# In each attention step of the first block, VectorE reads out the finished head and copies the turned probabilities ahead of the row maximum of the step's scores

## The reference

```
h = rms_norm(x); proj = h @ w_in
6 heads:  softmax(q k^T / 8 + c[t] - c[s]) v          (forget gates, causal)
4 heads:  (softmax(q1 k1^T) - lam softmax(q2 k2^T)) v (causal)
6 heads:  softmax over the 128 keys with the largest index score, times a shared v
x = x + concat(heads) @ w_out
x = x + (silu(h' @ w_gate) * (h' @ w_up)) @ w_down,   h' = rms_norm(x)
```

## Time and profile before

| | |
|---|---|
| median of 3 runs | 2273.99 us (2273.98 to 11201.12) |
| profiled execution | 2271.32 us, its span 2269.5 us |
| PE busy | 2063.1 us, 91% of the span |
| DVE / ACT / POOL busy | 1230.1 / 854.6 / 518.6 us |
| mean granted PE clock | 0.952 of full speed |
| attention steps, first layer | about 102 to 391 us |
| attention steps, second layer | about 862 to 1152 us |

### The profile page before, as it was taken

One profiled execution on the slowest core, in us unless ns is written; L12 is line 12 of the kernel. 1 busy time (PEld: TensorE's weight loads), 2 busy tenths in 40 slices (PEclk: granted clock), 3 DMA queues, 4 the chain that ended last, 5 costly groups with the idle time before them and its releaser, 6 DMA issues. The chain is left out here.

```text
span 2269.5 us, 30334 instructions
## 1 busy us (share of the span) xinstructions
PE 2063.1 (91%) x11592; PEld 1760.0 (78%) x11592; DVE 1230.1 (54%) x2338; ACT 854.6 (38%) x1402; POOL 518.6 (23%) x355
## 2 busy tenths in 40 slices
PE   6988898899999999798989999999799989789994
PEld 6887777788888788786768888888788878777773
DVE  3676453544454447745554444538962233479885
ACT  4444433421222344343442212214224552267762
POOL 2654321000000136532110000004365535200001
PEclk9999988999999999898989999999999999799997
DMA  4111100412221111110123122205346543489995
GB/s 154 57 57 38 42 25 19 176 59 108 111 103 64 38 61 57 38 38 28 38 99 133 63 104 111 100 11 160 72 124 190 153 139 112 166 326 404 402 380 214
DMA packets 61627, 270.95 MB, mean 119 GB/s; under 512 B 15040, under 2 KB 19904, under 8 KB 37056
## 3 DMA queue, kind: packets, MB, share of 16 engines
q1 hardware_dynamic: 52864, 237.84, 30.1%
q10 hardware_dynamic: 6048, 22.02, 2.5%
q0 software_dynamic: 2592, 9.44, 1.1%
HBM read 244.14 MB, written 37.19 MB: 124 GB/s over the span
## 5 line engine op out<-in xcount | busy, mean ns | idle before, releaser
L1241 PE MATMUL fill_ps<-w_hi,h_hi 128*128 128x256 f32 (+1 forms) x704 | 213.1, 303 | 13.9 <-ACT values L866 5.2
L1241 PE MATMUL fill_ps<-w_hi,h_lo 128*128 128x256 f32 (+1 forms) x704 | 203.7, 289 | 0.0
L1241 PE MATMUL fill_ps<-w_lo,h_hi 128*128 128x256 f32 (+1 forms) x704 | 203.2, 289 | 0.0
L795 POOL TENSOR_TENSOR w_lo<-w_raw,w_hi 128x1024 fp32r<-128x1024 f32 x60 | 151.7, 2539 | 193.5 <-ACT w_hi L858 192.7
L322 POOL TENSOR_SCALAR norm_ss<-norm_ss 128x1 f32<-128x1 f32 x24 | 4.9, 202 | 798.6 <-ACT ffn_raw_d L316 738.2
L516 DVE TENSOR_TENSOR ffn_silu<-ffn_silu,ffn_up 128x512 f32<-128x512 f32 x44 | 30.2, 687 | 285.9 <-ACT ffn_silu L474 285.9
L1241 PEld LDWEIGHTS fill_ps<-w_hi,h_hi 128*128 128x128 f32 x704 | 140.6, 200 | 27.1 <-issue 16.1
L528 DVE TENSOR_TENSOR x<-ffn_down,x 128x512 f32<-128x512 f32 x176 | 119.1, 689 | 71.2 <-PE ffn_down L590 70.4
L1321 PEld LDWEIGHTS o_ps<-values,prob_t 128*128 128x128 f32 x800 | 111.7, 201 | 57.4 <-DVE prob_t L1100 46.9
L1707 POOL TENSOR_TENSOR w_lo<-w_raw,w_hi 128x1024 fp32r<-128x1024 f32 x48 | 126.0, 2642 | 131.3 <-ACT w_hi L1814 131.3
L575 PE MATMUL ffn_up<-h_hi,w_hi 128*128 128x512 f32 x384 | 152.1, 396 | 3.7 <-PEq L772 3.7
(11 more groups left out here) (456 smaller groups left out, 5651.4 us busy)
## 6 DMA issues: line engine op xcount, KB each, us to landing
moe_raw_gu<-in_w_e_gu SPq DMA_DIRECT2D x46, 1024.0 KB, 12.0
w_raw<-in_w_mix SPq DMA_DIRECT2D x28, 1024.0 KB, 5.0
w_raw<-in_w_two SPq DMA_DIRECT2D x23, 1024.0 KB, 5.1
moe_raw_d<-in_w_e_down SPq DMA_DIRECT2D x23, 1024.0 KB, 8.3
w_raw<-in_w_gate SPq DMA_DIRECT2D x22, 1024.0 KB, 5.8
w_raw<-in_w_up SPq DMA_DIRECT2D x22, 1024.0 KB, 6.7
ffn_raw_d<-in_w_down SPq DMA_DIRECT2D x22, 1024.0 KB, 5.0
moe_in<-in_zero SPq DMA_DIRECT2D x23, 512.0 KB, 7.7
```

The costliest lines, as they stand in the source:

```text
L795: nc.gpsimd.tensor_tensor(w_lo[s][:, cols], w_raw[s][:, cols], w_hi[s][:, cols].bitcast(F32), ALU.subtract).then_inc(lo_done, 1)
L1241: last = nc.tensor.matmul(b[:, 0:cols], aw[:, k, t * P:(t + 1) * P], ww[:, k, 0:cols], start=k == 0 and n == 0, stop=k == KD - 1 and n == 2)
```

## The change

Three calls on VectorE stand in another order within a step. Nothing is added or removed, and the streams of the other engines are the same.

```diff
                 for n in range(LAST + 1):
+                    if n >= 7 and n % TB == 3 and n < STEPS + 4:
+                        store((n - 7) // TB)
+                    if 2 <= n < STEPS + 2 and (n - 2) % TB < 2:
+                        copy_pt(n - 2)
                     if n < STEPS:
                         score_max(n)
-                    if 2 <= n < STEPS + 2 and (n - 2) % TB < 2:
-                        copy_pt(n - 2)
-                    if n >= 7 and n % TB == 3 and n < STEPS + 4:
-                        store((n - 7) // TB)
                     if n in TURN_AT:
```

## The result

The changed kernel takes 2243.14 us (median of 4 runs, 2237.29 to 2244.74) against 2273.98 of the kernel before: a ratio of 0.9876, 95% interval 0.9856 to 0.9897. The forecast was 2236, with 2222 to 2262 around it. Two more sets of runs of the same kernel gave 2239.09 us (ratio 0.9851, 0.9833 to 0.987) and 2241.04 us (0.9873, 0.9858 to 0.9888). So it is 1.2 to 1.5% faster, clear of no change and short of 2%. The profiled execution has a span of 2240.9 us, 28.6 less than before.

The account below looks back on a forecast made before the run. PE was taken to set the pace in the attention, with idle time and half clock winnable. Pauses 21.6 us plus clock 16.4 made 38 off 2271.3, 2233; with the median 2.7 above the profiled run, 2236 us, range 2222 to 2262.

Parts of the forecast that it names:

- What PE waits for: Step 67: PE's first value matmul waits 1.72 us for the old head's store on VectorE, not the copy the profile names.
- Price of a pause: Ahead of PE's value matmuls: a pause costs idle time plus 0.16 us; 1.9 each in three steps, 10.8 us a layer.
- correction of 0.16 for modelled ends: Modelled matmul ends make a pause 0.16 us longer than its idle time; eight such corrections add 1.3 us a layer.
- Step 15: VectorE is late with norms; PE goes on 0.94 us earlier, counted as 0.47 because it runs at half clock.
- Steps 19, 39 and 47 give their gain back: VectorE is late there; PE's gains, some 1.2 us at 19 and at most 0.94 at 47, count 0.
- The clock: Half clock behind steps 35, 55, 67 and 79 comes from the pauses; 8.2 us a layer return, 16.4 in all.
- thin work: Stretch from 305 to 316, behind step 55: sparse PE work may hold half clock, so 2.5 of 5.1 us was counted.
- The reading against the forecast: By the Trainium skill alone, thin stretches stay at half clock without the pause; 21.6 us won instead of 38.
- a sign of being wrong: Half clock stretches appearing where there were none; a fall elsewhere was put at 1.6 to 3.3 us.
- the clock staying low: Rival: pauses go, but half clock remains for want of activity; 2252 us, chance 0.18.
- more coming through: Rival: late steps keep their gain and every low clock stretch goes; 48 us won, 2226 us, chance 0.15.
- a new wait for `exp` in steps 57, 69 or 81: Rival: PE's next wait, for ScalarE's exponential, takes over; only three long pauses a layer are won, 2263 us, chance 0.13.

Follow-up runs that it names:

- experiment 3: Kernel before the change, with store and copy ahead of the maximum in steps 55, 67 and 79 alone: 2244.44 us, ratio 0.9897.
- experiment 4: Kernel before the change, old order kept, with eight extra 128x512 matmuls on PE in the pauses of steps 55, 67 and 79: 2251.38 us, ratio 0.9919.
- experiment 5: Changed kernel with the old order put back in steps 19, 39 and 47: 2241.45 us, ratio 0.9852.
- The version with this split: Changed kernel with the stores of steps 15 and 47 moved behind the maximum of steps 14 and 46, ahead of norm and search work: 2226.47 us, ratio 0.9798.

## Why the prediction was right, step by step

- *What PE waits for*: right. The store is the releaser; moving the copy alone leaves a wait of 1.39.
- *Price of a pause*: right in the main, some 15% too high. With the clock loss taken off, the attention went from 264.3 to 254.4 and from 263.9 to 255.0 us, 9.9 and 8.9 against 10.8 forecast. In experiment 3 the three long pauses alone gave 4.0 us of the first layer (264.3 to 272.2 - 11.9 = 260.3) for the 5.7 counted; where the rest stays is not shown. The correction of 0.16 for modelled ends was about right at step 67, where 2.10 became 0.33 from score to value; I had expected 0.25.
- *Step 15*: the wait fell from 6.88 to 6.02, by 0.86 for the 0.94 forecast.
- *Steps 19, 39 and 47 give their gain back*: right, at the places named. The wait behind step 19 rose from 1.89 to 2.93, VectorE's L1025 now holds PE for 0.87 at 250.62, and the addition to x for 1.50 at 279.49 instead of 0.28 of a weight load. With the old order restored there, the waits of steps 39 and 47 have nearly the same sum. Step 39 takes back more than its own gain: PE now waits 1.15 + 0.87 us there instead of 0.39, so part of what the steps before it won goes too.
- *The clock*: the mechanism was right, the close sum in part luck. In the first profile it is 8.5 us a layer for 8.2 forecast, but terms were off and cancelled. In the first layer the stretch behind step 55 came back whole, 5.1 and not 2.5, which speaks against thin work as its cause, and so did the one behind step 35, 1.7 and not 0.8. Against that stand new losses: behind the longer wait at 188.67 half clock held for 5.1 us of loss instead of 3.4, and 1.7 us were lost from 109 on, before the change acts. Over both layers the clock loss fell by 17.0, 10.2 and 16.9 us in the three profiles, for 16.4 forecast. Of the Trainium skill's sentence (TensorE: Matmul & The Clock Gate, Part 1), that throttled is the default and activity releases it, the runs agree with the part on activity: extra matmuls alone kept 2.4 GHz in experiment 4. The reading against the forecast, half clock without any pause, did not come true in these three places.
- *The total*: 28.6 us of span for 38 forecast. The attention gave 35.8, and 7.3 us are clock loss in stretches that the change does not touch. A second profile of the same kernel had none of that, but there the attention gave only 30.0. The weak term is one that I did not have: half clock elsewhere I named only as a sign of being wrong, and that sign did appear, though each fall in the attention here cost 1.7 us or more, and the times of one kernel spread by 7 to 13 us. By the medians, 31, 32 and 29 us below the kernel before.
- *Rivals*: the clock staying low is refuted by experiments 3 and 4; more coming through, by the waits of experiment 5; a new wait for `exp` in steps 57, 69 or 81 did not appear.

## What to carry to other kernels

In a stream that runs in order, put what another engine waits for ahead of what has slack, and ahead of any instruction that must itself wait for that engine; look in the code for the real releaser, since the row can name a neighbour. Price a short pause of PE by its length and by the half clock that follows it: here three pauses of 1.9 us, with what followed them, cost 14.3 us of a layer, about 10 of it clock. Before counting a late engine's gain, follow PE to its next wait for that engine; if the work up to there is the same, the gain is given back.

## What the runs showed of the hardware that I had not expected

- Pauses of 1.72 us of recorded idle time were followed by about 3 to 10 us at 1.2 GHz though PE was then busy all the time, and eight needless matmuls in each such pause made the kernel 17 us faster.
- The same program lost 7 us more to half clock outside its attention in one profile than in another, and its executions ranged from 2230.16 to 2244.74 us over the three sets.
- With one wait of 6.02 us split into 0.55, 2.43 and 0.83, the half clock behind it cost 1.7 us instead of 3.4 or more, in both layers. The version with this split gained mostly through the clock (attention less clock loss 254 to 255 us either way).
